# Hybrid decoder trunk: split output projection, value products of two heads on the halves of the output rows

## The reference, cut to what matters

```python
def block(args):                      # group A, per block of 128 queries
    ...                               # indexer scores, top_k keys, ALiBi
    p = jax.nn.softmax(logits, axis=-1).astype(v.dtype)
    return jnp.einsum('bhqk,bqkhd->bqhd', p, v_sel)      # value product, 8 heads x 64

def step(S, xs):                      # group B, chunkwise gated recurrence
    ...
    return S, inter + intra

...
o_b = rms_norm(o_b, ...) * jax.nn.silu(...)              # 8 heads x 64
o = jnp.concatenate([o_a.reshape(B, L, A_WIDTH), o_b.reshape(B, L, B_VAL_WIDTH)], axis=-1)
return o @ w_out                                          # 1024 x 1024
h = layer_norm(ALPHA * h + mix, ...)
```

## Time and profile before

| what | value |
|---|---|
| median of 3 runs | 2518.83 us (2517.43 to 2522.06) |
| profiled execution, its own time | 2517.84 us |
| its span, first to last instruction | 2516.0 us |
| PE busy, share of the span | 2440.6 us, 97% |
| DVE, ACT, POOL busy | 1185.0, 962.2, 1051.7 us |
| mixers stage, about | 467 to 931 us |
| all `w_out_part` matmuls | 480 records of 240 matmuls |

### The profile page before, as it was taken

How to read it: one execution, slowest core, us unless ns; L and a number is a source line. 1 busy time by engine, 2 the same in 40 slices (tenths; PEclk the granted TensorE clock), 3 DMA queues, 4 the chain that set the end, 5 groups by cost and what they waited for, 6 DMA issues and landing times.

```text
span 2516.0 us, 35675 instructions
## 1 busy us (share of the span) xinstructions
PE 2440.6 (97%) x13796; PEld 2100.7 (83%) x13796; DVE 1185.0 (47%) x2304; ACT 962.2 (38%) x1630; POOL 1051.7 (42%) x584
## 2 busy tenths in 40 slices
PE   7899999989999989999999999999999999999996
PEld 7889999768888779899998888888888888888885
DVE  6788985445555423333333465323365432232224
ACT  3677783344444224222223433322333322332222
POOL 0433123365544324443443544544444444455432
PEclk9999999899999999999999999999999999999998
DMA  4101330334332334333232323233233333333331
GB/s 140 34 18 35 99 101 31 105 98 130 106 117 90 97 107 120 93 101 93 76 101 84 100 78 107 84 117 92 76 101 101 91 94 101 101 101 105 113 101 42
DMA packets 275000, 231.40 MB, mean 92 GB/s; under 512 B 10768, under 2 KB 255568, under 8 KB 274832
## 3 DMA queue, kind: packets, MB, share of 16 engines
q1 hardware_dynamic: 266640, 220.59, 29.2%
q10 hardware_dynamic: 8192, 8.52, 1.0%
HBM read 215.81 MB, written 12.71 MB: 91 GB/s over the span
## 4 chain that ended last, share of the span: by engine, by line
PE 60%; DMA 1%; ACT 1%; POOL 1%; DVE 1%; issue 0%; POOLq 0%; SPq 0%; ACTq 0%; DVEq 0%
PE banks L2056 38%; PE banks L2090 19%; PE banks L2122 1%; PE banks L1777 1%; DMA last_draw<-in_w_down 0%; PE banks L2081 0%; PE banks L2084 0%; POOL dL L1999 0%; PE banks L2108 0%; DMA cq_raw<-in_w_up 0%; POOL wL L1992 0%; ACT dH L2174 0%; DVE y L2314 0%; ACT hH L1787 0%; DVE n_bn L1686 0%
## 5 line engine op out<-in xcount | busy, mean ns | idle before, releaser
L1992 POOL TENSOR_TENSOR wL<-cq_raw,wH 128x2048 fp32r<-128x2048 f32 x87 | 406.6, 4673 | 528.7 <-ACT wH L2168 528.7
L2056 PE MATMUL banks<-hL,wH 128*128 128x512 f32 (+1 forms) x1760 | 618.9, 352 | 5.5 <-ACT hid L2183 2.8
L2056 PE MATMUL banks<-hH,wL 128*128 128x512 f32 (+1 forms) x1760 | 618.0, 351 | 0.0
L2056 PE MATMUL banks<-hH,wH 128*128 128x512 f32 (+1 forms) x1760 | 616.0, 350 | 0.0
L2056 PEld LDWEIGHTS banks<-hL,wH 128*128 128x128 f32 x1760 | 331.1, 188 | 54.7 <-ACT hid L2183 3.7
L2288 DVE TENSOR_TENSOR hid<-hid,banks 128x512 f32<-128x512 f32 (+1 forms) x110 | 64.3, 584 | 656.8 <-PE banks L2056 560.5
L2056 PEld LDWEIGHTS banks<-hH,wL 128*128 128x128 f32 x1760 | 331.1, 188 | 46.4
L2056 PEld LDWEIGHTS banks<-hH,wH 128*128 128x128 f32 x1760 | 331.8, 189 | 44.9
L1999 POOL TENSOR_TENSOR dL<-last_draw,dH 128x1024 fp32r<-128x1024 f32 x88 | 220.7, 2508 | 311.6 <-ACT dH L2174 311.6
L2314 DVE TENSOR_TENSOR y<-y,banks 128x512 f32<-128x512 f32 (+1 forms) x340 | 232.0, 686 | 183.4 <-PE banks L2090 182.1
L2174 ACT ACTIVATE dH<-last_draw 128x1024 fp32r<-128x1024 f32 x88 | 93.3, 1061 | 496.6 <-PE banks L2090 320.6
(11 more groups left out here) (278 smaller groups left out, 4128.8 us busy)
## 6 DMA issues: line engine op xcount, KB each, us to landing
cq_raw<-in_w_gate SPq DMA_DIRECT2D x88, 512.0 KB, 4.5
cq_raw<-in_w_up SPq DMA_DIRECT2D x88, 512.0 KB, 6.0
last_draw<-in_w_down SPq DMA_DIRECT2D x88, 512.0 KB, 3.4
w_out_part<-in_w_out SPq DMA_DIRECT2D x60, 512.0 KB, 4.1
va<-in_w_in SPq DMA_DIRECT2D x10, 1024.0 KB, 5.4
va<-in_x SPq DMA_DIRECT2D x8, 512.0 KB, 4.7
vg_scratch<-y ACTq DMA_DIRECT2D x32, 128.0 KB, 1.7
y<-in_x SPq DMA_DIRECT2D x8, 512.0 KB, 8.5
```

Source lines behind the costliest of these rows:

```text
L1992: nc.gpsimd.tensor_tensor(wL[:, ff % 2, :, :, :].rearrange("p g k f -> p (g k f)"), raw[:, :, :, :].rearrange("p g k f -> p (g k f)"), wH[ ...
L2056: last = nc.tensor.matmul(banks[:, GU + (2 * q + g) % 3, 0:n], wt[:, ff % 2, g, k, :], h[:, k, a:a + n], start=(k == 0 and part == 0), sto ...
```

## The change

The output projection of tiles 0 to 7 becomes three fp32r matmuls for each float32 one: low part of `o` by high part of `w_out`, high by low, high by high (24 per quarter). The weights are split in the first stage, in eight chunks that ScalarE rounds, GpSimd subtracts and ScalarE's queue stores to a scratch tensor; the mixers stage loads 1024 KB for each half of a quarter instead of 512 KB. `o` is split as it leaves the shared bank: two ScalarE copies (`oH`), two VectorE subtractions (`oL`). The last tile's quarters stay float32.

The value product is turned round: the values of a head are the weights (64 columns), the turned probabilities move (128 columns), and two heads go to the rows 0 to 63 and 64 to 127 of the bank, in one job for two heads at odd `h`. The result is already turned, so `ot_att` goes. The inverse sums, which now differ along the columns, are spread by eight matmuls against the identity (`share`, at the start of step 2), copied out by ScalarE, and multiplied by VectorE. The buffer of turned probabilities keeps two slots; its slot is free again when the pair's job is done. The first quarter moves from `h` = 7 to `h` = 0 of the next tile. The recurrence's gate is applied at `h` = 3, its norm at `h` = 4. Two buffers are shared: `q_past` with `u`, and the last `oT` half with `probs`.

```diff
+    OUT_WITH = 5
+    first_unit = [min(i for i, u in enumerate(slab_units) if u[0] == j) for j in range(len(SLABS))]
+    split_after = [first_unit[OUT_WITH - 3 + c // 2] + 2 + c % 2 * 2 for c in range(len(OUT_CHUNKS))]
+    assert split_after[-1] < first_unit[OUT_WITH + 1]
+
     def slab_part(n):
 
         u, k = divmod(n, DC)
         order.append(("slab", u, k))
         if k == DC - 1:
             order.append(("out", u))
+            if u in split_after:
+                order.append(("w_out", split_after.index(u)))
+            if u - 1 in split_after:
+                order.append(("w_out_store", split_after.index(u - 1)))
...
+            if what == "w_out":
+                act.wait_ge(wo_loaded[m % 2], 16 * (m // 2 + 1))
+                nc.scalar.activation(out_part(m)[:, 0, :].bitcast(F32R), out_part(m)[:, 1, :], ACT.Copy).then_inc(wo_hi, 1)
+            if what == "w_out_store":
+                act.wait_ge(wo_lo, m + 1)
+                act.dma_start(wo_dram[OUT_CHUNKS[m]], out_part(m)).then_inc(wo_stored[m % 2], 16)
...
     def shared_job(m, h):
-        jobs = {0: ("meta", m - 1), 1: ("out", m - 1), 2: ("kT", m - 1), 3: ("state", m - 1), 4: ("qa", m + 1), 5: ("ot_att", m - 1),
-                6: ("ot_rec", m - 1)}
+        jobs = {0: ("meta", m - 1), 1: ("out", m - 1), 2: ("kT", m - 1), 3: ("state", m - 1), 4: ("qa", m + 1), 6: ("ot_rec", m - 1)}
         if m == NT and h in (2, 3):
             return None
         return jobs[h] if h in jobs and 0 <= jobs[h][1] < NT else None
 
+    def share_job(m, h):
+
+        return m - 1 if h == 2 and 1 <= m <= NT else None
+
     def out_job(m, h):
 
-        jobs = {7: (m - 1, 0), 1: (m - 2, 1), 3: (m - 2, 2), 5: (m - 2, 3)}
+        jobs = {0: (m - 2, 0), 1: (m - 2, 1), 3: (m - 2, 2), 5: (m - 2, 3)}
         if h not in jobs or not 0 <= jobs[h][0] < NT:
             return None
         t, q = jobs[h]
         return (t, LAST_ORDER[q]) if t == NT - 1 else (t, q)
...
                 if job and kh == 1:
                     sp.wait_ge(shared_psum, nth["op", (job - 1) // 4, (job - 1) % 4])
-                q = job % 4
-                sp.dma_start(wq[:, kh, :, :], w_v[:, kh * 4:kh * 4 + 4, q * QW:(q + 1) * QW]).then_inc(wq_loaded[kh], 16)
+                sp.dma_start(wq[:, kh, :, :, :].rearrange("p a k f -> p a (k f)").bitcast(F32), wo_dram[job % 4, kh]).then_inc(wq_loaded[kh], 16)
...
             if (m, h) == (NT, 2):
-                sp.wait_ge(pv_done, turned_to(NU - 1))
-            if m == NT and h in (0, 2):
-                for q in LAST_ORDER[h:h + 2]:
-                    sp.dma_start(wq_last[q], w_v[:, :, q * QW:(q + 1) * QW]).then_inc(wl_loaded[q], 16)
+                sp.wait_ge(pv_done, pairs_to(NU - 1))
             if out_job(m, h):
                 t, q = out_job(m, h)
-                if t < NT - 1 and 4 * t + q + 1 < 4 * (NT - 1) - 2:
+                if 4 * t + q + 1 < 4 * (NT - 1):
                     load_w(4 * t + q + 1)
+            if m == NT and h in (1, 3):
+                for q in LAST_ORDER[h - 1:h + 1]:
+                    sp.dma_start(wq_last[q], w_v[:, :, q * QW:(q + 1) * QW]).then_inc(wl_loaded[q], 16)
...
+            if what == "share":
+                pe.wait_ge(rs_done, m + 1)
                 for f in range(4):
-                    last = nc.tensor.transpose(banks[:, SHARED, f * P:f * P + n], o_tok[0:n, s, f * P:(f + 1) * P],
-                                               ident[0:n, 0:n])
+                    for par in range(2):
+                        share = rsums[0:n, s, 2 * f + par:2 * f + par + 1].to_broadcast([n, HD])
+                        last = nc.tensor.matmul(banks[HD * par:HD * (par + 1), SHARED, f * P:f * P + n], share, ident[0:n, 0:n],
+                                                start=True, stop=True)
...
-                if kept_quarter(m, q):
-                    w = wq_last[q][:, k, :]
+                if m == NT - 1:
                     if k == 0:
                         pe.wait_ge(wl_loaded[q], 16)
-                else:
-                    w = wq[:, k // 4, k % 4, :]
-                    if k % 4 == 0:
-                        pe.wait_ge(wq_loaded[k // 4], 16 * (4 * m + q + 1))
-                last = nc.tensor.matmul(banks[0:n, bank, 0:QW], oT[:, m % 2, k, 0:n], w, start=(k == 0), stop=(k == DC - 1))
+                    last = nc.tensor.matmul(banks[0:n, bank, 0:QW], (oT_rec if k // 4 else o_att)[:, k % 4, :], wq_last[q][:, k, :],
+                                            start=(k == 0), stop=(k == DC - 1))
+                    continue
+                if k % 4 == 0:
+                    pe.wait_ge(wq_loaded[k // 4], 16 * (4 * m + q + 1))
+                for part, (o, w) in enumerate(((oL, 0), (oH, 1), (oH, 0))):
+                    last = nc.tensor.matmul(banks[0:n, bank, 0:QW], o[:, k, 0:n], wq[:, k // 4, w, k % 4, :],
+                                            start=(k == 0 and part == 0), stop=(k == DC - 1 and part == 2))
...
-        def pv(i):
+        def pv_pair(i):
             m, h = units[i]
+            f = h // 2
             pe.wait_ge(t_act, turned_to(i))
             if dve_turns(i):
                 pe.wait_ge(t_dve, dve_turns(i))
-            if h == 0:
+            if f == 0:
                 pe.wait_ge(otok_done, m)
             for j in range(1, m + 1):
-                last = nc.tensor.matmul(banks[:, PV, h * HD:(h + 1) * HD], pT[:, i % 2, j, :],
-                                        va[:, j, h * HD:(h + 1) * HD], start=(h == 0 and j == 1), stop=False)
+                for par in range(2):
+                    last = nc.tensor.matmul(banks[HD * par:HD * (par + 1), PV, f * P:(f + 1) * P],
+                                            va[:, j, (2 * f + par) * HD:(2 * f + par + 1) * HD], pT[:, (i - 1 + par) % TS, j, :],
+                                            start=(f == 0 and j == 1), stop=False)
             last.then_inc(pv_done, 1)
...
-            if A_HEADS + 2 <= i <= NU + 1:
-                pv(i - 2)
+            if A_HEADS + 2 <= i <= NU + 1 and (i - 2) % 2:
+                pv_pair(i - 2)
...
-            if turned_to(i - 2):
-                act.wait_ge(pv_done, turned_to(i - 2))
+            if pairs_to(i - TS):
+                act.wait_ge(pv_done, pairs_to(i - TS + (i - TS + 1) % 2))
...
+            if what == "share":
+                if m:
+                    act.wait_ge(shared_done, nth["ot_rec", m - 1])
+                ins_ = nc.scalar.activation(o_att[:, :, 0:n], four(src)[:, :, 0:n], ACT.Copy)
...
+                    act.wait_ge(otok_done, m + 1)
+                    if m:
+                        act.wait_ge(shared_psum, nth["op", m - 1, 3])
+                    for half in range(2):
+                        nc.scalar.activation(oH[:, 4 * half:4 * half + 4, 0:n], o_columns(half, n), ACT.Copy).then_inc(o_hi, 1)
+                    return
...
+        def inverted(m):
+            n = TILES[m][1]
+            dve.wait_ge(exp_done, A_HEADS * (m + 1))
+            if m >= 2:
+                dve.wait_ge(shared_psum, nth["share", m - 2])
+            nc.vector.reciprocal(rsums[0:n, m % 2, :], sums[0:n, m % 2, :]).then_inc(rs_done, 1)
 
         def normed(m):
             n = TILES[m][1]
-            dve.wait_ge(exp_done, A_HEADS * (m + 1))
-            nc.vector.reciprocal(rsums[0:n, m % 2, :], sums[0:n, m % 2, :]).then_inc(rs_done, 1)
-            dve.wait_ge(rs_done, m + 1)
             dve.wait_ge(meta_done, m + 1)
-            if m >= 2:
-                dve.wait_ge(shared_psum, nth["ot_att", m - 2])
-            nc.vector.tensor_tensor(o_tok[0:n, m % 2, :].rearrange("p (h e) -> p h e", h=A_HEADS),
-                                    banks[0:n, PV, :].rearrange("p (h e) -> p h e", h=A_HEADS),
-                                    rsums[0:n, m % 2, :].rearrange("p (h e) -> p h e", e=1).to_broadcast([n, A_HEADS, HD]),
-                                    ALU.mult).then_inc(otok_done, 1)
+            dve.wait_ge(shared_done, nth["share", m])
+            nc.vector.tensor_tensor(o_att[:, :, 0:n], o_att[:, :, 0:n], four(banks[:, PV, :])[:, :, 0:n], ALU.mult).then_inc(otok_done, 1)
...
+        def o_low(m):
+            n = TILES[m][1]
+            for half in range(2):
+                dve.wait_ge(o_hi, 2 * m + half + 1)
+                at = slice(4 * half, 4 * half + 4)
+                last = nc.vector.tensor_tensor(oL[:, at, 0:n], o_columns(half, n), oH[:, at, 0:n].bitcast(F32), ALU.subtract)
+            last.then_inc(shared_done, 1)
...
+                dve.wait_ge(gated, m)
+                linked(nc.vector.tensor_tensor(on[:, :], on[:, :], gt[:, :], ALU.mult))
             if h == 4 and 1 <= m <= NT:
                 dve.wait_ge(rsh_done, m)
                 on8 = on[:, :].rearrange("p (h e) -> p h e", h=8)
-                linked(nc.vector.tensor_tensor(on8, on8, rsh[:, :].rearrange("p (h e) -> p h e", e=1)
-                                               .to_broadcast([P, 8, HD]), ALU.mult))
```

(56 more changed lines are left out.)

48 lines of the change are left out of this document (30 added, 18 removed).

## The result

The changed kernel takes 2547.32 us (median of four runs, 2545.13 to 2552.82), the kernel before 2519.26 us: 1.0116 times as long, 95% interval 1.0104 to 1.0128. It is 28 us slower. The direction was forecast, the size was not: 2527 us, and 2547.3 lies just beyond the range.

A forecast was written before the change was run, and what follows sets the result against it. TensorE, busy for 97% of the span, was taken to bound the kernel. Against the profiled 2517.84 us, savings of 22.4 and 22.6 us and added costs, mostly waits, summed to +9.4, so 2527 us; range 2507 to 2547.

The forecast's parts named there:

- term 4: First quarter behind `meta` at tile boundaries: waits for ScalarE's copy, held back by GpSimd's chain; +30 us, from +7 to +40.
- Quarters: Output projection's 32 split quarters: 2.81 us each instead of 3.51; −22.4 us, at worst 0.
- Value products: Paired value products on two output halves run together, with 0.24 us overhead a job; −22.6 us, from −30.5 to +8.
- the rival without overlap: Value products on output halves do not run together, so term 2 is +8; about 2553 us, chance 0.13.
- Share: Inverse sums spread in nine tiles: +5.9 work, +4.8 waits for VectorE's addition, −2.1 waits gone; together +8.6 us.
- GpSimd's pace: Short steps in tiles 2 to 5: TensorE waits again for GpSimd's carry; +3.3 us, from 0 to +10.
- Last tile: Two more VectorE subtractions ahead of the masks, for which the last logits wait; +3 us, 0 to +6.
- Weights: End of tile 7: larger loads for its last quarter land late; +9 us, from 0 to +14.
- the rival with late weights in small tiles: Quarters 0 and 1, one short step apart, wait for loads in small tiles too; about 2539 us, chance 0.15.
- First stage: Splitting the weights on ScalarE and GpSimd lies beside a busy TensorE; put at nothing, 0 to +3 us.
- The faster rival: Boundary wait mostly hidden, `meta` copied within 1 us of its end, term 4 is 8; about 2505 us, chance 0.25.

The follow-up runs named there:

- the filled run: Changed kernel plus unread matmuls behind `meta` at the boundaries of tiles 2 to 8, quarter 0 still at step 0: 2538.31 us, ratio 1.0074 to the kernel before.
- copy first: Changed kernel, quarter 0 still at step 0, with ScalarE copying `meta` out before the join and the turned probabilities: 2516.73 us, ratio 0.9993 to the kernel before.
- the two changed kernels with tiles 0 and 1 filled: Changed kernel with quarter 0 at step 7, kaT loads last and 33 unread matmuls: 2503.53 us; with the inverse sums' spread also later: 2501.18 us.

## Why the prediction was wrong

**The step that failed** is the sum's treatment of a wait: term 4 has "**+30 us**" for idle time alone, and none of the eight terms has the clock. The earlier trace rows showed it at 0.98 in a stage that hardly waits, and the prediction took that as given for a stage with 47 us more idle time. It fell in the mixers stage and cost 17.1 us more than before: 12.5 behind the boundary waits of tiles 2 to 7, 2.0 behind the 6.9 us at the end, and 2.6 at tiles 0 and 1, where the stretch at the lower clock from 487 us is 17 us long and not 10. The 2527 plus 17 is 2544, three below the measured median. In the ledger the stage is 22 us longer than the sum had it: these 17.1, and 6.2 of work that was not saved, less 1.3 of idle time. That the idle time comes out to 1.3 us is partly luck: the boundary waits are 4.8 us less than reckoned, and where −2.1 stands for small waits that go, new ones came: the turning jobs, which waited for nothing before, wait 4.4 us in ten waits, 3.4 of them for the copies of the turned probabilities.

By its own steps:

1. *Quarters* (−22.4). A quarter takes 2.98 us, not 2.81; in the ledger's terms the 36 quarters went from 126.8 to 108.3 us, −18.5. The size was off: 0.117 a matmul was read where one long stream of them ran; inside a quarter it is 0.120 (three in 0.36 us), and about 0.1 us a quarter comes on top.
2. *Value products* (−22.6). Right: ten matmuls take 729.68 − 728.44 = 1.24 us, and all of them 36.5 us where 61.8 were, −25.3.

```profile
728.44 1.31 PE L1377 MATMUL banks<-pT,va 128*64 128x128 f32 x20
...
729.68 1.58 PE L1307 MATMUL banks<-kaT,qaT 128*128 128x512 f32 x4
```

The halves of the output rows do overlap, as those of the input rows, and the rival without overlap falls. The overhead of a job was taken too high, 0.24 us against 0.15 (below).
3. *Share* (+5.9 work, +4.8 wait). +4.6 and 4.7.
4. *Boundary* (+30). 25.2 us in eight waits: 5.2, 4.2, 3.7, 3.4, 2.5, 2.5 and 3.0 at tiles 2 to 8, where 5.8, 5.2, 4.4, 3.9, 3.6, 2.7 and 3.2 were reckoned, and 0.8 in the last tile for 1.2. The idle time is right in place, cause and order of size; what it does to the clock is the failed step above. The argument that GpSimd stands behind ScalarE held at tile 6 too, though in the kernel before the join there began 3.4 us after the carry.
5. *GpSimd's pace* (+3.3). The waits for the carry rose from 7.4 to 10.8 us: +3.4.
6. *Last tile* (+3). Not told apart; the waits for the masks rose by 2.1 us over the whole stage.
7. *Weights* (+9). 10.5 us, in three waits of 1.85, 1.75 and 6.91.

```profile
928.90 0.36 PE L1299 MATMUL banks<-w_out_part,oL 128*128 128x256 f32 x1 [1.85 <-DMA w_out_part<-w_out_split]
...
932.32 0.38 PE L1299 MATMUL banks<-w_out_part,oL 128*128 128x256 f32 x1 [1.75 <-DMA w_out_part<-w_out_split]
...
940.92 0.55 PE L1299 MATMUL banks<-w_out_part,oL 128*128 128x256 f32 x1 [6.91 <-DMA w_out_part<-w_out_split]
```

No wait for them stands anywhere else in this profile (the filled run has one of 1.3 us, at 589 us), so the rival with late weights in small tiles falls.
8. *First stage* (0). TensorE is busy for all of 405 to 465 us, as before.

Missing from the list was also a cost of 3.8 us of work in the turned probabilities (32.2 to 36.0 us for 64 jobs, 0.06 us each) and 2.5 us spread over the other jobs. Half of the turning jobs run beside a pair with another tiling, but no run here takes that apart. Nor is it shown why the two changed kernels with tiles 0 and 1 filled have a stretch of 14 us at the lower clock near 890 us, in tile 8, that the others lack.

The faster rival's condition did not hold: the mean wait at tiles 2 to 8 is 3.5 us and not 1. But it priced the right place: where an edit takes the wait away, the kernel is at 2512.8 (quarter moved back) or 2516.7 (copy first), on the other side of before or level with it. It gave 2505 without a clock term; that 4.6 us more are lost to the clock than before even at 2512.8, and that the quarters save 4 us less, is about the difference.

## What to carry to other kernels

Before a saving on the bounding engine is added up, follow who waits for whom across the place that is moved: a job that shares a bank must wait for the read-out of the job ahead, and that read-out for everything its engine does first, here an operation that waits for a third engine. Price a wait of some microseconds on a TensorE that is otherwise hardly idle (23 of 465 us) at more than its length: here 47 us of added waits cost 64. And try the parts of a large change apart: one line of this one cost 35 us and hid what the rest gained.

## What the runs showed of the hardware

- Seven waits of 2.5 to 6.9 us between full work (those at tiles 2 to 7, and the long one for weights) each brought 3.4 to 6.8 us at half the granted clock, beginning in the wait or up to 1.1 us behind it, and at tile 6 three of the quarter's matmuls then took 0.64 us where they took 0.36 before. The wait at tile 8, 2.96 us, brought none in this profile and 3.4 us in the second one of the same kernel. Shorter waits are not safe either: in the kernel before with the quarter moved, waits of 1.45 and 1.50 us (at tile 8 and at 944 us) were followed by 3.4 us at the lower clock, those of 1.43 and 1.24 us at tiles 6 and 7 were not. So these runs give no length below which a wait is free. Matmuls that nobody reads, put in the wait, kept the clock at 1.00 (the filled run against the changed kernel: 10.5 us).
- Two float32 matmuls on the halves of the output rows overlap almost fully. In tile 8, 16 matmuls of 128 columns take 894.82 − 892.92 = 1.90 us, 0.119 each, against 0.212 for one on all columns of the array. That is 1.8 times the rate; the Trainium skill, "TensorEngine Tiling (Array Packing)", Theoretical Speedup, has up to 2, and the trace agrees. Short jobs get less of it: a job of 2, 10 and 16 matmuls takes 0.37, 1.24 and 1.90 us, so 0.15 us and 0.109 for each matmul, and for two matmuls that is 1.15 times the rate.
- The last two loads of 1024 KB, issued while the last tile's weights were loaded as well, took 10.1 and 9.2 us to land; the median of all 64 is 5.3.
